# Stick-breaking attention in blocks of 127 keys, with the running sum carried in row 0

## The reference: what is computed

```
z = einsum('bqhd,bkhd->bhqk', q_blk, kh) * scale
mask = key_pos[None, :] < q_pos[:, None]
log_1m_beta = where(mask, log_sigmoid(-z), 0.0)
between = cumsum(log_1m_beta, axis=3, reverse=True) - log_1m_beta
weights = where(mask, exp(log_sigmoid(z) + between), 0.0)
out = einsum('bhqk,bkhd->bqhd', weights, vh)
```

## Time and profile before

| | |
|---|---|
| timed runs | 1551.15, 1556.61, 1557.23 us |
| profiled execution | 1550.32 us, span 1548.5 us |
| TensorE busy | 1466.1 us, 95% |
| VectorE busy | 670.5 us, 43% |
| ScalarE busy | 525.2 us, 34% |
| GpSimd busy | 308.9 us, 20% |
| mean granted clock of TensorE | 0.987 |

### The profile page before, as it was taken

How to read it: one execution, slowest core, us unless ns; L and a number is a source line. 1 busy time by engine, 2 the same in 40 slices (tenths; PEclk the granted TensorE clock), 3 DMA queues, 4 the chain that set the end, 5 groups by cost and what they waited for, 6 DMA issues and landing times.

```text
span 1548.5 us, 27297 instructions
## 1 busy us (share of the span) xinstructions
PE 1466.1 (95%) x11281; PEld 1138.3 (74%) x11281; DVE 670.5 (43%) x1072; ACT 525.2 (34%) x947; POOL 308.9 (20%) x412
## 2 busy tenths in 40 slices
PE   7989989989898899999999999999999999999997
PEld 5767777767677555554777788888888888888876
DVE  6244151555653454655464424242332424242337
ACT  5423231433323476877443403021120403021132
POOL 6674615422332252523001000000000000000000
PEclk9999989999999999999999999999999999999999
DMA  6454413423224513021433302021120302111014
GB/s 201 138 149 120 127 42 97 125 59 86 70 68 109 166 25 78 6 76 62 163 109 109 109 0 95 14 68 41 38 70 0 98 10 75 34 57 51 27 60 171
DMA packets 134969, 124.10 MB, mean 80 GB/s; under 512 B 20829, under 2 KB 112154, under 8 KB 134874
## 3 DMA queue, kind: packets, MB, share of 16 engines
q1 hardware_dynamic: 88588, 92.90, 19.4%
q10 hardware_dynamic: 46286, 29.84, 6.8%
HBM read 97.88 MB, written 24.84 MB: 79 GB/s over the span
## 4 chain that ended last, share of the span: by engine, by line
PE 47%; DVE 2%; ACT 1%; DMA 1%; issue 1%; POOLq 0%; SPq 0%; DVEq 0%; ACTq 0%
PE all_ps_b L2018 22%; PE all_ps_b L1995 22%; PE all_ps_b L1585 2%; DMA bk_acc<-in_w_out 1%; POOLq L1605 0%; DVE bk_acc L1872 0%; PE all_ps_b L1988 0%; ACT bk_acc L1773 0%; DVE bk_acc L1882 0%; DVE bk_w1L L1843 0%; DVE bk_acc L1868 0%; DVE all_hL L1888 0%; DVE all_gL L1914 0%; ACT bk_rect L1804 0%; DVE bk_acc L1945 0%
## 5 line engine op out<-in xcount | busy, mean ns | idle before, releaser
L1924 DVE TENSOR_TENSOR bk_acc<-bk_acc,all_ps_b 128x512 f32<-128x512 f32 x128 | 87.9, 687 | 274.4 <-PE all_ps_b L2018 274.2
L1995 PE MATMUL all_ps_b<-all_hH,bk_w1L 128*128 128x512 f32 x512 | 200.2, 391 | 5.1 <-PE all_ps_b L2018 2.1
L2018 PE MATMUL all_ps_b<-bk_w2H,all_gL 128*128 128x512 f32 x512 | 199.4, 389 | 2.5 <-DVE all_gL L1914 2.5
L1995 PE MATMUL all_ps_b<-all_hH,bk_w1H 128*128 128x512 f32 x512 | 199.4, 389 | 0.0
L1995 PE MATMUL all_ps_b<-all_hL,bk_w1H 128*128 128x512 f32 x512 | 199.3, 389 | 0.0
L2018 PE MATMUL all_ps_b<-bk_w2L,all_gH 128*128 128x512 f32 x512 | 199.2, 389 | 0.0
L2018 PE MATMUL all_ps_b<-bk_w2H,all_gH 128*128 128x512 f32 x512 | 199.2, 389 | 0.0
L1207 PE MATMUL fr_ps_F<-fr_hH,fr_wL 128*128 128x512 f32 (+1 forms) x416 | 174.7, 420 | 6.5 <-POOL fr_wL L459 6.4
L459 POOL TENSOR_TENSOR fr_wL<-fr_raw,fr_wH 128x256 fp32r<-128x256 f32 (+1 forms) x208 | 161.9, 809 | 26.0 <-ACT fr_wH L504 22.7
L1207 PE MATMUL fr_ps_F<-fr_hL,fr_wH 128*128 128x512 f32 (+1 forms) x416 | 164.8, 396 | 0.0
L1207 PE MATMUL fr_ps_F<-fr_hH,fr_wH 128*128 128x512 f32 (+1 forms) x416 | 164.5, 395 | 0.0
(11 more groups left out here) (349 smaller groups left out, 2281.9 us busy)
## 6 DMA issues: line engine op xcount, KB each, us to landing
fr_raw<-in_w_in ACTq DMA_DIRECT2D x37, 512.0 KB, 4.2
bk_raw<-in_w_ff SPq DMA_DIRECT2D x32, 512.0 KB, 4.3
all_raw<-in_w_ff SPq DMA_DIRECT2D x32, 512.0 KB, 3.7
projected<-fr_stage ACTq DMA_DIRECT2D x39, 256.0 KB, 4.4
fr_raw<-in_w_in SPq DMA_DIRECT2D x13, 512.0 KB, 4.3
fr_xt<-in_x SPq DMA_DIRECT2D x8, 512.0 KB, 5.1
bk_acc<-in_x SPq DMA_DIRECT2D x8, 512.0 KB, 3.3
x_after_mixers<-bk_acc SPq DMA_DIRECT2D x8, 512.0 KB, 2.6
```

The costliest lines, as they stand in the source:

```text
L1924: dve.tensor_tensor(acc[:, j, ds], acc[:, j, ds], ybank[g % 4][:], ALU.add).then_inc(collected, 1)
L1995: m = pe.matmul(bank[s][h][:], w[s][:, k, :], a[:, k, hs], start=(k == 0 and q == 0), stop=(k == KB - 1 and q == 2))
L2018: m = pe.matmul(ybank[g % 4][:], a[:, i, ts], w[:, i, ds], start=(i == 0 and q == 0), stop=(i == FB - 1 and q == 2))
```

## The change

Blocks now hold 127 keys, on partitions 1 to 127. Partition 0 belongs to the sum of the later blocks. The loads leave column 0 of every block of 128 columns free in the keys and values (`load_blocks`), and ScalarE sets those columns to zero once (`clear`), so row 0 of a block's scores starts at 0. The masks are rebuilt in `front`: `later` is the triangular matrix with a row 0 of ones, so that whatever stands in row 0 of SP is added to every row of Z, and to row 0 too; `later_only` has zeros in that row, for columns that no later block has reached. Row 0 of Z, after `sums`, is the negative sum over this block and all later ones. ScalarE copies it behind the weight into `row` (`hand_on`), and GpSimd lays it into row 0 of the SP of the same head's next block. The matrix `ones`, the tiles R and GpSimd's additions are gone.

1024 keys make nine blocks of 127, where there were eight: a pair now has 10 units in half 0 and 18 in half 1, the new ones 4 and 8 columns wide. The mask matmul was in float32r (one instruction) and is now in float32 (two).

```diff
-SB_MASKS = ("ones", "to_diag", "above", "same64")
+SB_MASKS = ("same64", "never", "later", "later_only")
+KEYS, KCOLS = P - 1, TB * P + 16
+    def clear(self, act, ident):
+        for t in self.kd:
+            act.activation(t[:, USED - 1:USED], ident[:, 0:1], ACT.Copy, scale=0.0)
+        for t in self.kd + [self.vp]:
+            last = act.activation(t[:].rearrange("p (b c) -> p b c", c=16)[:, 0::P // 16, 0],
+                                  ident[:, 0:TB + 1], ACT.Copy, scale=0.0)
+        return last
+    def load_blocks(self, q, to, rows, src, done):
+        whole = TB * KEYS
+        q.dma_start(to[rows, 0:TB * P].rearrange("p (b c) -> p b c", c=P)[:, :, 1:P],
+                    src[:, 0:whole].rearrange("p (b c) -> p b c", c=KEYS)).then_inc(done, 16)
+        q.dma_start(to[rows, TB * P + 1:TB * P + 1 + T - whole], src[:, whole:T]).then_inc(done, 16)
...
-        for kb in range(PER * (c + 1) - 1, -1, -1):
+        top = ((c + 1) * HALF - 1) // KEYS
+        for b in range(top, -1, -1):
             for h in range(2):
-                UNITS.append((h, c, kb, max(0, (kb - PER * c) * P), kb == PER * (c + 1) - 1))
+                UNITS.append((h, c, b, max(0, (KEYS * b - c * HALF) // 2 * 2), min(P, (c + 1) * HALF - KEYS * b + 1), b == top))
...
 GpSimd
-                            pool.tensor_tensor(new[:, off:], old[:, off:], SP[u % 4][:, off:], ALU.add
-                                               ).then_inc(s("sum"), 1)
-                        if off:
-                            pool.memset(new[:, off - P:off], 0.0)
...
+                    if not first:
+                        known = UNITS[u - 2][3]
+                        pool.wait_ge(s("handed"), handed(i, u - 2))
+                        pool.wait_ge(s("sp"), i * NU + u + 1)
+                        pool.tensor_copy(SP[u % 4][0:1, known:HALF], row[(u - 2) % 4][0:1, known:HALF]
+                                         ).then_inc(s("placed"), 1)
+                        gla(i * NG + NTH[u] - 1)
...
 ScalarE
+                def hand_on(u):
+                    off = UNITS[u][3]
+                    if u >= 4 and hands_on(u - 4):
+                        act.wait_ge(s("placed"), placed(i, u - 2))
+                    act.copy(row[u % 4][0:1, off:HALF], Z[u % NZ][0:1, off:HALF]).then_inc(s("handed"), 1)
                 for u in range(NU):
                     weight(u)
+                    if hands_on(u):
+                        hand_on(u)
...
 TensorE, scores
                     pe.wait_ge(s("weight"), i * NU + u - NZ + 1)
+                    if u >= NZ and hands_on(u - NZ):
+                        pe.wait_ge(s("handed"), handed(i, u - NZ))
...
-                    m = pe.matmul(Z[u % NZ][:, off:off + P], unit[:], never[:], start=False, stop=True,
+                if masked > 0:
+                    m = pe.matmul(Z[u % NZ][0:rows, off:off + masked], ident[0:rows, 0:rows],
+                                  mask["never"][0:rows, low:low + masked], start=False, stop=True, skip_group_check=True)
...
 TensorE, sums
-                    m = pe.matmul(z, tri[:], SP[u % 4][:, span(u)], start=False, stop=True, skip_group_check=True)
-                    if not first:
-                        pe.wait_ge(s("cut"), i * NU + u - 1)
-                        m = pe.matmul(z, ones[:], rd[:, span(u)], start=False, stop=True, skip_group_check=True)
+                    if off < known:
+                        m = pe.matmul(z[0:rows, off:known], mask["later_only"][0:rows, 0:rows], sp[0:rows, off:known],
+                                      start=False, stop=True, skip_group_check=True)
+                    if known < HALF:
+                        pe.wait_ge(s("placed"), placed(i, u))
+                        m = pe.matmul(z[0:rows, known:HALF], mask["later"][0:rows, 0:rows], sp[0:rows, known:HALF],
+                                      start=False, stop=True, skip_group_check=True)
```

More of the change, by code:

```diff
@@ L2117, in heads @@
     NZ, AHEAD = 4, 3
+    END = [sum(1 for x in UNITS if x[1] <= c) for c in range(QC)]
+    NTH = [sum(1 for x in UNITS[0:n] if not x[5]) for n in range(NU + 1)]
+    NG = NTH[NU]
+    TURNS = (range(1, 5), (0, 5, 6, 7), (8,))
+    VALUES_READY = [1 + max([n for n in range(3) if any(x[2] in TURNS[n] for x in UNITS[0:u + 1])]) for u in range(NU)]
     with ExitStack() as st:
         r = Region(nc, st, "sb")
[L2120 removed]
+        r.sb("early", [P, early.size])
         qd, kd, vp, kS, qH, qL = early.qd, early.kd, early.vp, early.kS, early.qH, early.qL
[L2122 removed]
+        vn = r.sb("vn", [P, TB + 1, P])
         E = [r.sb(f"E{n}", [P, HALF]) for n in range(4)]
         SP = E
[L2125 removed]
+        row = [r.sb(f"row{n}", [1, HALF]) for n in range(4)]
         W = [r.sb(f"W{n}", [P, HALF]) for n in range(4)]
[L2127 to L2128 removed]
+        eps = r.sb("eps", [P, 1])
         O, osq = [r.sb(f"O{n}", [P, T]) for n in range(2)], r.sb("osq", [P, T])
@@ L2567, in sum_bank, with part, handed, hands_on @@
             return G[0] if i == LAST and n else X
-        def span(u):
-            h, c, kb, off, first = UNITS[u]
-            return slice(off, HALF)
+        def part(t, u):
+            h, c, b, off, rows, first = UNITS[u]
+            return t[0:rows, off:HALF]
+        def handed(i, u):
+            return i * NG + sum(1 for n in range(u + 1) if hands_on(n))
+        def hands_on(u):
+            return u + 2 < NU and not UNITS[u + 2][5]
+        def placed(i, u):
+            return i * NG + NTH[u + 1]
         def half(n):
@@ L2723, in _ @@
         def _(dve):
-            dve.tensor_copy(unit[:], ident[:])
-            dve.tensor_scalar(never[:], mask["above"], -1.0, FAR, ALU.add, ALU.mult).then_inc(s("far"), 1)
-            dve.tensor_scalar(tri[:], mask["to_diag"], -1.0, None, ALU.mult)
-            dve.tensor_scalar(ones[:], mask["ones"], -1.0, None, ALU.mult).then_inc(s("signs"), 1)
             def split(i):
@@ L2837, in scores @@
-                m = pe.matmul(Z[u % NZ][:, span(u)], kS[h][:, kb * P:(kb + 1) * P], qH[h][:, qs], start=False, stop=True)
-                if kb >= PER * c:
-                    if not i and u == 0:
-                        pe.wait_ge(s("far"), 1)
-                    m = pe.matmul(Z[u % NZ][:, off:off + P], unit[:], never[:], start=False, stop=True,
-                                  skip_group_check=True)
+                z, k = Z[u % NZ][0:(rows + 1) // 2 * 2, off:HALF], kS[h][:, b * P:b * P + (rows + 1) // 2 * 2]
```

166 lines of the change are left out of this document (79 added, 87 removed).

## The result

The changed kernel takes 1563.49 us (median of 20 runs, 1556.62 to 1569.28) against 1556.15 us of the kernel before (20 runs beside them): ratio 1.0046, 95% interval 1.003 to 1.0062. It is 7 us slower. The forecast was 1547 us; the time lies outside the range of 1532 to 1562 and on the other side of the old time.

A forecast was written before the change was run, and what follows sets the result against it. TensorE, busy 95% of the span, was taken as the bound, passing to ScalarE in half 1. From 1550.3 us, minus 7 (half 1) plus 1 (half 0) gave about 1544, put at 1547 us against the timed median; range 1532 to 1562.

The forecast's parts named there:

- What TensorE sheds and gets: Heads stage: `ones` gone saves 43.9 us, masks, cut `sums` and new units add 17; TensorE 204.4 to 177.5 us.
- What ScalarE gets: Heads stage: 72 one-row copies, 22 us, and 12 new units, 4.4 us; ScalarE 157.2 to 184 us.
- The row's path: Heads stage, `sums` through weight and both row copies to `sums`(u+2): 4.2 us per two full-width units, against 5.67 today.
- The first rival: Before `sums`(u+2), GpSimd's row copy waits behind GLA work or VectorE; path 6.4 us, total 1559 us; chance 0.14.
- How far the bound is reached: Heads stage: near-level TensorE and ScalarE reach 93% of the bound; half 1 wins 7 us, half 0 loses 1.
- rival 2: Half 1 of heads: ScalarE takes the whole gain back, 140 us as now, total 1552 us; chance 0.11.
- The clock: Heads stage: TensorE gaps bring four more clock dips and waits, 5 to 8 us on top, total 1553 us; chance 0.08.
- Rivals 2 and 4: Heads stage: ScalarE takes all the gain back (1552 us, chance 0.11); TensorE gaps lower its clock (1553 us, chance 0.08).
- Front: Before heads: 14 early DMAs for 9 and five clearing operations cost nothing; without the cover, up to 3 us.
- Good hiding (rival 3): Heads stage: TensorE's stalls hide well and ScalarE waits only where it must; 18 us won, total 1536 us; chance 0.22.

The follow-up runs named there:

- The short copies: The changed kernel with ScalarE's row copy cut to the last 4 columns, GpSimd's copy and all waits kept: 1552.95 us, ratio 0.9973 to the kernel before.
- The two gap runs: Four idle matmuls filling TensorE's gap at pair 1's end in the changed kernel: 1559.59 us; three unused ScalarE copies lengthening that gap in the kernel before: 1562.11 us.

## Why the prediction was wrong

**What TensorE sheds and gets: too good.** Its busy time in the stage fell by 15.2 us (202.1 to 186.9), where my sum had 26.9 (204.4 to 177.5). Some 5 us of the difference can be the 10 us more at 1.2 GHz, where records are longer. The rest is in the terms. `ones` is worth 0.75 to 0.8 us at 512 columns and not 0.86: for instance, from the start of `sums` to that of the second `scores` matmul it is 1.95 us with it (645.94 to 647.89) and 1.20 without (577.71 to 578.91). The masks went from 6.4 to 16.5 us, start to next start, 10 us more for the 7.2 that I took: I had counted 48 and there are 60. The cut of `sums` in two costs little: 0.22 us from L2893 to L2897 for 126 columns, which is the columns' own time. The `later` matmul of a full-width unit stands alone, as forecast.

**What ScalarE gets.** Right: 72 copies, 558 ns at 512 (forecast 0.57), no rebate for one partition, 179.8 us busy (forecast 184).

**The row's path.** Right: TensorE waits 1.8 us for GpSimd's copies (forecast under 5). The first rival's mechanism did show, though. Four of the 72 copies took over 0.9 us, each begun while VectorE was at an operation with two SBUF inputs. One of 390 columns took 1.16 us and ended 0.37 us after VectorE's; one of 386 at 687.57 us, with nothing beside it, took 0.50:

```profile
711.59 1.21 DVE L1605 TENSOR_TENSOR all_hL<-early_qd,all_hH 128x1024 fp32r<-128x1024 f32 x1
...
712.01 1.16 POOL L2660 COPY sb_E<-sb_row 1x390 f32<-1x390 f32 x1 [2.02 <-ACT sb_row L2717]
```

The Trainium skill, "SBUF — State Buffer" (Who interferes with whom), says that a VectorE instruction with two SBUF inputs contends with a GpSimd instruction that reads SBUF; the trace agrees. But TensorE seldom waits for GpSimd's copies.

**"How far the bound is reached": the step that failed.** I gave the three halves 1 minus 5, minus 1 and minus 1 us. They changed by -4.7, +3.0 and +3.4. I took the fuller engine of each, TensorE or ScalarE, and 93% of it.

- Pair 0: right. TensorE is busy 43.6 of 46.67 us, 93%.
- Pair 2: the rule held and its input was wrong. ScalarE is busy 39.4 of 42.60 us, 93%. But I had read the stretch of before from 687 to 733 us, which holds 4.4 us of half 0 and 2.4 us of `back`. Between its own ends half 1 took 39.18 us with 32.7 of ScalarE's work; 6.4 more is 39.1, and at 93% that is 42 us. By my own rule this half had to get 3 us longer.
- Pair 1: the rule itself failed. ScalarE is busy 47.2 of 55.40 us, 85%. It splits the next keys and queries late, TensorE's gap at the pair's end grew from 1.25 to 3.84 us, and the clock fell to 0.95. With the gap filled the half is 1.6 us shorter.

The rule also makes work on the less full engine free. The short copies say otherwise for pair 0: 4.3 us off ScalarE, the less full one by a little, gave 1.7. That a unit goes back and forth between the engines and that neither can run ahead by more than a unit would explain it, but this is argued and not shown. The outcome is what rival 2 said (ScalarE takes all of it back, 1552), at 0.11.

**The clock: the second step.** It was a rival at 0.08, priced at four dips, 5 to 8 us. The kernels' means are 23 us at 1.2 GHz apart. At 0.32 us each, the slope among runs, that is 7 us, and at 0.4, what the pairs of profiles with and without a dip show (3.0 for 7 us, 2.7 for 7, 1.4 for 3.4), 9 to 10. The two gap runs show the direction and a part of the size. What I had in hand and weighed too little was the earlier trace rows, a dip behind gaps at 604, and the 33 us of ScalarE's waits that were TensorE's cover: when ScalarE waits for TensorE, TensorE has few gaps. The change turned that round: TensorE stood idle 7 us of the stage and now 26. The chance for the clock should have hung on this, not stood beside it. The Trainium skill, "TensorE: Matmul & The Clock Gate" (A second HAM failure mode), tells of short idle gaps between groups of matmuls. The trace agrees with it only in part: gaps of 1.1 to 1.2 us in half 1 of pair 2 left the clock at 1.00. Rivals 2 and 4 were priced as alternatives and came together: 1552 + 7 is 1559.

**The sum of the miss.** Of 16.5 us 3 are the base: the forecast leaned on the profiled execution, which lacks the dip at the start of the stage. Some 7 to 10 us are the clock. At the clock of before the change would be about level, where I had 6 us won. What is left, 3 to 6 us, lies in half 1 of pairs 1 and 2 and in TensorE's terms.

**Front: nothing.** Right: three more constants change nothing that the runs can tell, and the old front's starts spread over 4.5 us. The early loads were not tried by themselves.

**Other forecasts.** The weights' wait for `sums` was to be 10 to 18 us and is 7.0: the sign was right, and the low figure says that ScalarE is later than I thought. Heads ended at 736.8 us, not 725. Late row (rival 1): no. Good hiding (rival 3): no.

## What to carry to other kernels

Read each engine's load between a stage's own ends, not between round numbers: 7 us of neighbours hid that the last half had no room for the added work. Where two engines hand each unit back and forth, price added work by stretch. Here it cost its whole length where its engine alone was nearly full (pair 2), 0.4 of it where both were (pair 0), and 0.1 to 0.3 in the old kernel, where the other engine was full: never nothing. Before taking work off TensorE, ask what keeps it busy: new gaps on it can lower its clock, and the loss comes behind the gap. Compare the mean clocks of all runs, not of one profile, before explaining a difference of half a per cent, and compare profiles stretch by stretch: where the clock agrees, one program's stretches agree to 0.02 us.
